# Moving modulation units, weight roundings and partial additions in a two-layer hybrid mixer block

## The chip, the cores and the metric

The kernel runs on one core of one Trainium2 chip. The metric is the device time of one execution in microseconds (us). A core has a matrix engine (PE, with its weight load PEld), a vector engine (DVE), a scalar engine (ACT), GpSimd (POOL) and a sync engine (SP) that here issues nearly all loads. Each engine executes its own instructions in order and waits at semaphores for the others.

## The reference, cut to what matters

Two layers run over 512 latent and 256 context tokens of width 1024. In each, a condition vector gives six modulation vectors by one large product; four mixers (differential attention DA, the gated recurrence HG, neighbourhood attention NA, windowed attention SW) take a quarter of the width each; their outputs go through `w_out`; a squared-ReLU MLP follows. All matrices are fp32.

```python
for layer in range(DEPTH):
    mod_l = adaln_params(c, w_mod[layer], b_mod[layer])      # silu(c) @ w_mod + b, split in 6
    p_l = split_cols(modulate(x, norm1_g[layer], mod_l[0], mod_l[1]) @ w_in[layer])
    ...                                                      # the same for the context
    a_l, a_c = diff_attention(...)                           # DA
    b_l, b_c = hgrn2_mixer(...)                              # HG, a scan over chunks of 64
    n_l, n_c = neighbourhood_attention(...)                  # NA
    w_l, w_c = window_gqa(...)                               # SW
    x = x + mod_l[2] * (jnp.concatenate([a_l, b_l, n_l, w_l], axis=-1) @ w_out[layer])
    x = x + mod_l[5] * squared_relu_mlp(modulate(x, norm2_g[layer], mod_l[3], mod_l[4]), ...)
```

Within HG a step of the scan needs, for 64 positions, scores with a decay `exp(cum[t] - cum[s])` inside each chunk, and the state product `k * exp(last - cum)` against the values:

```python
new_state = exp(last)[..., None] * state + einsum('bhsk,bhsv->bhkv', kc * exp(last[:, :, None] - cum), vc)
rel = where(lower, cum[:, :, :, None, :] - cum[:, :, None, :, :], -inf)
scores = einsum('bhtk,bhsk,bhtsk->bhts', qc, kc, exp(rel))
```

## The kernel before, in words

**Units.** Weights are handled in units of 256 output columns (1 MB, 0.75 MB for the units of `w_out` named `outA`). All units stand in one list. A unit is loaded by SP into one of two `raw` buffers, by turns, so the load of a unit is issued when the unit two places ahead in the list is done with its buffer: a modulation unit when its product has run, a split unit when its low part is made. A split unit (all but the modulations) is rounded by ACT (`whi`, L1410), its rest is made by POOL (`wlo`, L775, or by DVE), and PE multiplies three times. ACT takes up each rounding at a point of its own instruction order, in `after_unit`, and there waits until the load has landed: everything behind it on ACT waits too.

**Modulation units.** `("mod", l, j, i)` is column block i of modulation j of layer l. Its `row` is 16 small PE matmuls (L918), DVE copies the result to `mrow` (L1908), its `turn` is 4 tiny matmuls (L923) and one addition on DVE (L1912). They are filler work: `fill_plan` deals them, with the chunks of the next mixer's projections, into the slots of a mixer. PE runs a slot's work within one step of that mixer; DVE and ACT have their parts at fixed points of theirs.

**DA** has a step for each of 24 units of attention in layer 0 (16 in layer 1), and one slot for each, with one more at the end. On PE a step is the scores of the next unit (L1096), the transposes of this one (L1113), the slot, and every second step the product with the values (L1133). After the last step ACT squares the output (`DA_y`, L1632), PE averages it (L1161), and ACT, DVE and PE norm it. In ACT's order the last two roundings of units that the slots let through stand ahead of these squares.

**HG** runs over tiles of 128 positions, 6 in layer 0 and 4 in layer 1. A tile has 6 levels (distances 1, 2, 4, ... 32) and a diagonal. For a level PE makes differences of `cum` (L1206, L1207), four levels ahead of where it stands; ACT takes their exponentials (L1721, two levels at once); DVE multiplies them with q (`HGx_qd`, L2313) and POOL with k (`HGx_kd`, L762); PE makes the scores (L1246); DVE masks them into `HG_at` (L2324). The exponentials have two rooms, each of two levels. A slot follows on PE behind the differences of each level. The roundings of the first two units of `w_out`, `outA` 0 and 1, are let through by the last two modulation rows of the slots, and ACT takes a slot up behind the exponentials of level (slot + 4) or (slot + 3).

**Behind the levels** PE multiplies with `outA` in chunks (L888 to L890; 512 and 256 columns by turns in layer 0, 512 in layer 1) that alternate between two banks of PSUM; DVE adds a finished chunk to `xT` (`add`, L2464) and so frees its bank. At the same time DVE makes, for each head h, `kdiff(h)` (L2369) and, after ACT's exponential (L1742), `kscale(h)` (L2375). PE transposes the scaled keys (L1279) once all four heads are done.

## Time and profile before

| | us |
|---|---|
| median of 3 runs | 2327.4 |
| lowest and highest of them | 2324.64, 2330.38 |
| the profiled execution, device time | 2326.89 |
| its span in the trace | 2325.1 |
| PE busy | 2087.4 (90%) |
| DVE, ACT, POOL busy | 1017.4, 785.0, 688.7 |

The profiled execution lies 0.5 us below the median, and 1.8 us of it lie outside its span. A row of the timeline has the start of an instruction (or of a run of equal ones) in us from the span's start, its duration in us, engine, line, operation, output and inputs, the count, and in square brackets how long the engine sat idle before it and what it waited for.

### The profile page before, as it was taken

What the parts mean: (1) busy time and instruction counts of PE and PEld (TensorE: products, weight loads), DVE (VectorE), ACT (ScalarE), POOL (GpSimd) and SP (SyncE); (2) the same over time, 40 slices, a digit from 0 to 9 for tenths busy, and PEclk for the clock granted to TensorE, in tenths of its full rate; (3) what the DMA queues carried; (4) which work ended last, traced back from release to release, by engine and by line L of the source; (5) the groups of instructions that cost most, each with busy time, mean ns of one, the idle gap of its engine ahead of it and who ended that gap; (6) DMA issues with size and microseconds to landing.
All of it is one profiled execution on the core that took longest, in us unless ns stands there. A gap on an engine that the chain in (4) does not pass through costs nothing.

```text
span 2325.1 us, 32051 instructions
## 1 busy us (share of the span) xinstructions
PE 2087.4 (90%) x13292; PEld 1743.4 (75%) x13292; DVE 1017.4 (44%) x1791; ACT 785.0 (34%) x1283; POOL 688.7 (30%) x567
## 2 busy tenths in 40 slices
PE   5799898879878899999999988998978888999998
PEld 3678786757667788888888876777767767778787
DVE  2545547844665641222213353445846755121222
ACT  1533323423425531222213153223434355232231
POOL 0231211010760223223232222223013713444542
PEclk9899998979999999999999998998989979999999
DMA  8220000551311111211212123010351312322222
GB/s 282 50 70 20 31 25 21 180 145 46 109 59 40 55 55 55 73 55 60 68 55 73 55 44 75 19 37 19 107 129 52 119 37 64 100 91 91 91 91 73
DMA packets 178352, 169.72 MB, mean 73 GB/s; under 512 B 29392, under 2 KB 174752, under 8 KB 178080
## 3 DMA queue, kind: packets, MB, share of 16 engines
q1 hardware_dynamic: 175840, 161.12, 22.6%
q10 hardware_dynamic: 2368, 6.55, 0.9%
q8 instruction: 106, 1.74, 0.3%
q14 instruction: 38, 0.31, 0.0%
HBM read 159.79 MB, written 2.10 MB: 70 GB/s over the span
## 4 chain that ended last, share of the span: by engine, by line
PE 74%; DVE 10%; ACT 6%; issue 4%; DMA 3%; POOL 2%; SPq 2%; DVEq 0%; ACTq 0%; POOLq 0%
PE gp L864 52%; PE sp L1096 3%; POOL HGx_kd L762 2%; PE gp L1133 2%; PE tp L1113 1%; SPq L710 1%; DVE small L2165 1%; PE sp L1087 1%; PE gp L888 1%; PE sp L1246 1%; ACT nt L1444 1%; PE gp L918 1%; PE sp L937 1%; PE sp L997 1%; DMA raw<-in_w_mod 1%
## 5 line engine op out<-in xcount | busy, mean ns | idle before, releaser
L775 POOL TENSOR_TENSOR wlo<-raw,whi 128x512 fp32r<-128x512 f32 x386 | 511.4, 1356 | 1338.6 <-ACT whi L1410 1338.4
L864 PE MATMUL gp<-xhi,whi 128*128 128x512 f32 (+1 forms) x1424 | 521.8, 366 | 36.2 <-DVE xlo L1954 21.4
L864 PE MATMUL gp<-xhi,wlo 128*128 128x512 f32 (+1 forms) x1424 | 507.8, 357 | 0.0
L864 PE MATMUL gp<-xlo,whi 128*128 128x512 f32 (+1 forms) x1408 | 504.2, 358 | 0.0
L864 PEld LDWEIGHTS gp<-xhi,whi 128*128 128x128 f32 x1424 | 278.0, 195 | 84.1 <-issue 11.3
L1410 ACT ACTIVATE whi<-raw 128x2048 fp32r<-128x2048 f32 (+1 forms) x100 | 187.2, 1873 | 401.6 <-PE gp L864 356.4
L864 PEld LDWEIGHTS gp<-xhi,wlo 128*128 128x128 f32 x1424 | 277.1, 195 | 39.4
L864 PEld LDWEIGHTS gp<-xlo,whi 128*128 128x128 f32 x1408 | 274.4, 195 | 38.5 <-issue 2.0
L864 PE MATMUL gp<-hhi,whi 128*128 128x512 f32 (+1 forms) x768 | 276.8, 360 | 9.6 <-issue 5.0
L864 PE MATMUL gp<-hlo,whi 128*128 128x512 f32 (+1 forms) x768 | 275.2, 358 | 0.0
L864 PE MATMUL gp<-hhi,wlo 128*128 128x512 f32 (+1 forms) x768 | 274.8, 358 | 0.0
L2464 DVE SCALAR_TENSOR_TENSOR xT<-gp,mods,xT 128x512 f32<-128x512 f32 (+1 forms) x140 | 90.4, 654 | 374.7 <-PE gp L864 362.6
L2528 DVE TENSOR_TENSOR frel<-frel 128x512 f32<-128x512 f32 (+1 forms) x98 | 71.1, 726 | 244.4 <-ACT frel L1456 244.4
L864 PEld LDWEIGHTS gp<-hhi,whi 128*128 128x128 f32 x768 | 145.1, 189 | 37.0 <-DVE xT L2464 7.4
L864 PEld LDWEIGHTS gp<-hhi,wlo 128*128 128x128 f32 x768 | 145.2, 189 | 22.7
L864 PEld LDWEIGHTS gp<-hlo,whi 128*128 128x128 f32 x768 | 145.2, 189 | 22.2
L1456 ACT ACTIVATE frel<-gp 128x512 f32<-128x512 f32 (+1 forms) x98 | 50.5, 518 | 198.5 <-PE gp L864 198.5
L2165 DVE TENSOR_REDUCE small<-sp 128x1 f32<-128x768 f32 (+4 forms) x120 | 90.0, 792 | 42.4 <-PE sp L1096 42.4
L2530 DVE TENSOR_TENSOR hlo<-frel,hhi 128x512 fp32r<-128x512 f32 (+1 forms) x98 | 65.8, 671 | 60.7 <-ACT hhi L1873 60.7
L1246 PE MATMUL sp<-HGx_qd,HGx_kd 128*128 128x128 f32 x480 | 69.5, 290 | 19.1 <-DVE HG_at L2324 12.8
L1246 PEld LDWEIGHTS sp<-HGx_qd,HGx_kd 128*128 128x128 f32 x480 | 60.6, 198 | 29.5 <-issue 20.9
L1873 ACT ACTIVATE hhi<-frel 128x512 fp32r<-128x512 f32 (+1 forms) x98 | 54.3, 554 | 84.0 <-DVE frel L2528 84.0
(361 smaller groups left out, 3262.6 us busy)
## 6 DMA issues: line engine op xcount, KB each, us to landing
raw<-in_w_ff SPq DMA_DIRECT2D x64, 1024.0 KB, 5.3
raw<-in_w_mod SPq DMA_DIRECT2D x48, 1024.0 KB, 5.2
raw<-in_w_in SPq DMA_DIRECT2D x20, 1024.0 KB, 5.3
raw<-in_w_in SPq DMA_DIRECT2D x24, 256.0 KB, 4.8
bias<-e SPq DMA_DIRECT2D x96, 32.0 KB
raw<-in_w_out SPq DMA_DIRECT2D x12, 256.0 KB, 2.9
xin<-in_x ACTq DMA_DIRECT2D x1, 2048.0 KB, 9.9
raw<-in_w_out SPq DMA_DIRECT2D x16, 128.0 KB, 3.4
```

Source lines behind the costliest of these rows:

```text
L762: ins = nc.gpsimd.tensor_tensor(o, i0, dv[r, :, :, side, :], ALU.mult)
L775: nc.gpsimd.tensor_tensor(wlo[:, s % 2, ks, :], raw[:, index[splits[s]] % 2, ks, :], whi[:, s % 2, ks, :].bitcast(F32), ALU.subtract)\
L864: mm = pe.matmul(out, lhs, rhs, start=(i == 0 and j == 0), stop=(i == KT - 1 and j == 2))
L1096: mm = pe.matmul(region(m, n, j, o, o + w), ql if i == 2 else qh, kl if i == 1 else kh, start=(i == 0 and not added), stop=(i == 2))
L1246: mm = pe.matmul(sp_[:, idx % 2, P * h:P * h + P], kk, qq, start=True, stop=True)
L1410: nc.scalar.activation(whi[:, s % 2, 0:k_tiles(v), :], raw[:, index[v] % 2, 0:k_tiles(v), :], ACT.Copy)\
L1456: nc.scalar.activation(frel[:, e % 2, 0:b - a], bank(n)[:, 0:b - a], ACT.Relu).then_inc(bank_free[group_bank[n]], 1)
L1873: nc.scalar.activation(hhi[:, 2 * j + c[0], a:b], frel[:, e % 2, 0:b - a], ACT.Copy)\
L2165: V.tensor_reduce(small[:, c + j:c + j + 1], scored(m, n, j, w), AX.X, ALU.max, negate=True)\
L2464: ins = V.scalar_tensor_tensor(out=xT[:, k, a:b], in0=bank(n)[:, 0:b - a], scalar=mods[:, l, 8 * gate_chunk + k, MOD_COL[c[1]]:MOD_COL[c[1 ...
L2528: V.tensor_tensor(r, r, r, ALU.mult).then_inc(ls(l, "h_sq"), 1)
L2530: V.tensor_tensor(hlo[:, 2 * j + c[0], a:b], r, hhi[:, 2 * j + c[0], a:b].bitcast(F32), ALU.subtract)\
```

## The change

Three edits, no instruction added or taken away.

1. **The plan.** `counts` says how many modulation units each mixer's slots get. DA goes from 16 to 14 in layer 0 and from 9 to 7 in layer 1, HG from 8 to 10 and from 7 to 9.
2. **ACT's roundings in HG** follow their slot by 7 or 8 levels instead of 3 or 4, and what is left over is done at the end.
3. **DVE behind the levels** runs `add(0)` behind `kdiff(1)` instead of behind `kdiff(3)`, and, in layer 0, `add(1)` behind `kdiff(3)` instead of behind `kscale(3)`.

```diff
-    counts = {("NA", 0): 0, ("SW", 0): 0, ("DA", 0): 16, ("HG", 0): 8, ("NA", 1): 0, ("SW", 1): 0, ("DA", 1): 9, ("HG", 1): 7}
+    counts = {("NA", 0): 0, ("SW", 0): 0, ("DA", 0): 14, ("HG", 0): 10, ("NA", 1): 0, ("SW", 1): 0, ("DA", 1): 7, ("HG", 1): 9}
...
-                    if level >= 4:
-                        fill(ENDS["HG", l][level - 4])
-                        fill(ENDS["HG", l][level - 3])
+                    if level >= 8:
+                        fill(ENDS["HG", l][level - 8])
+                        fill(ENDS["HG", l][level - 7])
...
-                for slot in ENDS["HG", l][-5:]:
+                for slot in ENDS["HG", l][-9:]:
                     fill(slot)
...
                 kdiff(0)
                 kdiff(1)
+                add(0)
                 kscale(0)
                 kdiff(2)
                 kscale(1)
                 kdiff(3)
-                add(0)
+                if not last:
+                    add(1)
                 kscale(2)
                 kscale(3)
-                if not last:
-                    add(1)
```

What the plan gives, worked out from `fill_plan` (r is a row, t a turn, tok a chunk of 128 tokens of the projection HGi, which PE takes 24 matmuls for; a unit's turn stands in the slot behind its row, at its head):

| slots | before | after |
|---|---|---|
| DA 0, slots 21 to 24 | t r; t tok5; r; t r t | t r; t tok5 r; t r; t |
| DA 1, slots 13 to 16 | r; t tok5; r; t r t | the last eighth of tok4, r; t tok5 without its last eighth; that, r; t |
| HG 0, slots with rows | 0 3 6 10 13 16 20 23 | 0 2 5 8 10 13 16 18 21 24 |
| HG 1, slots with rows | 0 2 5 7 10 12 15 | 0 2 4 6 8 10 12 14 16 |

The units that follow DA's last two rows in the buffers are `HGf0` and `HGf1`, each loaded in four pieces of 64 columns. In layer 1 their loads are let go by the rows of slots 13 and 15, before by those of slots 15 and 16; in layer 0 by those of slots 22 and 23, before 23 and 24.

ACT in HG of layer 0, around levels 22 to 32. `whi` with 1536 columns is the rounding of `outA` 0 and then of `outA` 1, `mix<-tp` and `mix<-op` read the output of a finished tile out, `HG_tmp` and `HGx_exps` are the two rooms of the exponentials:

```order
 L1721 ACTIVATE HG_tmp<-sp,cf 128x2x2x128 x2
-L1410 ACTIVATE whi<-raw 128x1536
-L1721 ACTIVATE HGx_exps<-sp,cf 128x2x2x128 x2
-L1410 ACTIVATE whi<-raw 128x1536
+L1721 ACTIVATE HGx_exps<-sp,cf 128x2x2x128 x2
 L1712 ACTIVATE cum_hi<-sp 128x512
...
+L1410 ACTIVATE whi<-raw 128x1536
+L1721 ACTIVATE HGx_exps<-sp,cf 128x2x2x128 x2
+L1721 ACTIVATE HG_tmp<-sp,cf 128x2x2x128 x2
+L1410 ACTIVATE whi<-raw 128x1536
```

The first rounding moved from behind the exponentials of level 24 to behind those of 28, the second from 26 to 32. In layer 1 they go from 16 to 22, the last pair of levels, and from 18 to behind the last read-out.

ACT at the end of DA in layer 1; `whi` with 2048 columns is the rounding of `HGf0` and `HGf1`, `DA_pt` the copy of the last unit's transposes, `DA_y` the squares:

```order
 L1600 ACTIVATE DA_p,small<-sp,small 128x768 x2
-L1610 ACTIVATE DA_pt<-tp 128x384
-L1410 ACTIVATE whi<-raw 128x2048 x2
+L1410 ACTIVATE whi<-raw 128x2048
+L1610 ACTIVATE DA_pt<-tp 128x384
+L1410 ACTIVATE whi<-raw 128x2048
```

The rounding of `HGf0` moved ahead of the copy of the last transposes. In layer 0 ACT's order there is the same as before.

DVE behind the levels in layer 0; L2369 is `kdiff`, L2375 `kscale`, L2464 `add`:

```order
 L2369 TENSOR_TENSOR HG_tmp<-HG_cum,HG_ref 128x768 x2
+L2464 SCALAR_TENSOR_TENSOR xT<-gp,mods,xT 128x512
 L2375 TENSOR_TENSOR HG_k<-HG_k,HG_tmp 128x768
 L2369 TENSOR_TENSOR HG_tmp<-HG_cum,HG_ref 128x768
 L2375 TENSOR_TENSOR HG_k<-HG_k,HG_tmp 128x768
 L2369 TENSOR_TENSOR HG_tmp<-HG_cum,HG_ref 128x768
-L2464 SCALAR_TENSOR_TENSOR xT<-gp,mods,xT 128x512
+L2464 SCALAR_TENSOR_TENSOR xT<-gp,mods,xT 128x256
 L2375 TENSOR_TENSOR HG_k<-HG_k,HG_tmp 128x768 x2
-L2464 SCALAR_TENSOR_TENSOR xT<-gp,mods,xT 128x256
```

`add(0)` moved ahead by four instructions, `add(1)` by two.

## Rows read from the trace of the kernel before

**Rows 1.** The page, part 4: shares of the chain that ended last

```profile
PE 74%; DVE 10%; ACT 6%; issue 4%; DMA 3%; POOL 2%; SPq 2%; DVEq 0%; ACTq 0%; POOLq 0%
```

**Rows 2.** The timeline of PE, end of DA in layer 0

```profile
495.75 1.07 PE L918 MATMUL gp<-raw,silu_c 128*32 128x256 f32 x16
...
499.68 0.58 PE L923 MATMUL gp<-cf,mrow 128*128 128x2 f32 x4 [0.64 <-DVE mrow L1908]
511.22 5.25 PE L1161 MATMUL sp<-cf,DA_y 128*128 128x2 f32 x24 [10.97 <-ACT DA_y L1632]
```

**Rows 3.** The timeline of ACT, the same place

```profile
503.93 1.91 ACT L1410 ACTIVATE whi<-raw 128x2048 fp32r<-128x2048 f32 x1 [7.90 <-DMA raw<-in_w_in]
508.44 1.91 ACT L1410 ACTIVATE whi<-raw 128x2048 fp32r<-128x2048 f32 x1 [2.60 <-DMA raw<-in_w_in]
```

**Rows 4.** The timeline of SP (SPq), ends of DA in layers 0 and 1

```profile
496.88 14.36 SPq L721 DMA_DIRECT2D raw<-in_w_in  x9
...
1712.38 14.31 SPq L721 DMA_DIRECT2D raw<-in_w_in  x9
```

**Rows 5.** The timelines of PE and ACT, end of DA in layer 1

```profile
1701.37 1.07 PE L918 MATMUL gp<-raw,silu_c 128*32 128x256 f32 x16
...
1711.24 1.07 PE L918 MATMUL gp<-raw,silu_c 128*32 128x256 f32 x16
...
1719.37 1.91 ACT L1410 ACTIVATE whi<-raw 128x2048 fp32r<-128x2048 f32 x1 [7.86 <-DMA raw<-in_w_in]
...
1725.76 1.13 ACT L1632 ACTIVATE DA_y<-mix 128x512 f32<-128x512 f32 x2
```

**Rows 6.** The timeline of ACT, roundings among the levels, layers 0 and 1

```profile
652.74 1.48 ACT L1410 ACTIVATE whi<-raw 128x1536 fp32r<-128x1536 f32 x1 [2.89 <-DMA raw<-in_w_out]
...
661.73 1.48 ACT L1410 ACTIVATE whi<-raw 128x1536 fp32r<-128x1536 f32 x1 [6.35 <-DMA raw<-in_w_out]
...
1830.55 1.49 ACT L1410 ACTIVATE whi<-raw 128x1536 fp32r<-128x1536 f32 x1 [1.22 <-DMA raw<-in_w_out]
...
1837.02 1.48 ACT L1410 ACTIVATE whi<-raw 128x1536 fp32r<-128x1536 f32 x1 [3.31 <-DMA raw<-in_w_out]
```

**Rows 7.** The timeline of PE, what follows the second rounding, layers 0 and 1

```profile
665.20 2.05 PE L1246 MATMUL sp<-HGx_qd,HGx_kd 128*128 128x128 f32 x8 [5.90 <-DVE HG_at L2324]
...
1839.13 0.39 PE L1206 MATMUL sp<-dif,cum_hi 128*128 128x256 f32 x1 [1.17 <-ACT HG_tmp L1721]
```

**Rows 8.** The timeline of PE: first scores of tiles 0, 1, 3, 4, 5; layer 1: 0, 1

```profile
592.67 1.13 PE L1246 MATMUL sp<-HGx_qd,HGx_kd 128*128 128x128 f32 x8 [0.34 <-POOL HGx_kd L762]
...
606.92 1.06 PE L1246 MATMUL sp<-HGx_qd,HGx_kd 128*128 128x128 f32 x8
...
639.20 1.07 PE L1246 MATMUL sp<-HGx_qd,HGx_kd 128*128 128x128 f32 x8
...
657.77 1.06 PE L1246 MATMUL sp<-HGx_qd,HGx_kd 128*128 128x128 f32 x8
...
677.33 1.06 PE L1246 MATMUL sp<-HGx_qd,HGx_kd 128*128 128x128 f32 x8
...
1791.53 1.13 PE L1246 MATMUL sp<-HGx_qd,HGx_kd 128*128 128x128 f32 x8 [0.61 <-POOL HGx_kd L762]
...
1806.63 1.06 PE L1246 MATMUL sp<-HGx_qd,HGx_kd 128*128 128x128 f32 x8
```

**Rows 9.** The timelines of DVE and PE behind the levels, layer 0

```profile
696.70 0.96 DVE L2375 TENSOR_TENSOR HG_k<-HG_k,HG_tmp 128x768 f32<-128x768 f32 x1
...
700.43 0.75 DVE L2464 SCALAR_TENSOR_TENSOR xT<-gp,mods,xT 128x512 f32<-128x512 f32 x1
...
703.07 0.48 DVE L2464 SCALAR_TENSOR_TENSOR xT<-gp,mods,xT 128x256 f32<-128x256 f32 x1
...
701.23 0.80 PE L888 MATMUL gp<-mix_hi,whi 128*128 128x512 f32 x1 [4.91 <-DVE xT L2464]
...
707.33 0.60 PE L1279 MATMUL tp<-cf,HG_k 128*128 128x128 f32 x4
```

## The prediction, made before the changed kernel ran

> **What bounds the kernel now.** I read the chain that ended last first: 74% of it is PE and 10% DVE [rows 1]. So PE's own work decides nearly everywhere, and a change can pay in two ways: less PE work on the path, or fewer gaps on PE. Of the gaps I read the timelines of the three stretches that the diff touches, PE first and then the engine that it waited for.
>
> At the **end of DA** PE sits idle 10.97 us in layer 0 before the averages, waiting for ACT's squares [rows 2]. ACT had waited for two loads and rounded both units, and only then squares, from 508.44 + 1.91 = 510.3 [rows 3], though PE has no more attention to do from 500.3. The reader is to see a fixed sequence: row done (495.75 + 1.0), load issued at 496.88 [rows 4], landed at 503.93, which is 7.05 us after the issue, the next landed at 508.44, 4.51 later, its rounding 1.9, squares. In layer 1 it is the same: issue 1712.38, first landed 1719.37, squares 1725.76 [rows 4, 5]. **Among the levels** ACT waits for the loads of `outA` 0 and 1: 2.89 and 6.35 us in layer 0, 1.22 and 3.31 in layer 1 [rows 6]. The exponentials queued behind stop the levels, and after the second one PE has been idle 5.90 us and makes its 8 scores in 2.05 us instead of 1.06 [rows 7, 8]: they run at the clock's lower level, 1.2 GHz, after that idle time, the others at 2.4. **Behind the levels** in layer 0 PE waits 4.91 us for `add(0)`, which ends at 701.18, because its third chunk needs that bank [rows 9].
>
> **Part A, the end of DA in layer 0.** Removed are two units. A row takes 1.07 us and a turn 0.58 [rows 2], each with the end of its last matmul, which the next instruction overlaps; back to back I take 1.0 and 0.4, 2.8 for two units. Steps with a chunk in their slot are bound by PE, steps with a row alone partly by ACT and DVE, so not all of it counts: 2.8 less at most, some 2 at least. On the other side slot 22 now ends with a row, and DVE finishes the last unit's probabilities only after the chunk of that slot; this delays the last row, not the one before it. The load of `HGf0` goes out after the row of slot 22, which directly follows tok5; before, the last transposes stood between (0.3 us). So the issue comes 2.8 + 0.3 = 3.1 us earlier. The second load lands 4.5 us after the first wherever it is issued soon enough. Everything to the squares moves with it. **A = -3.0, between -2 and -4.** If the cover were gone (all of the removed work hidden anyway) it would be -0.3.
>
> **Part B, the end of DA in layer 1.** Here the load of `HGf0` is let go in slot 13, two steps earlier, and its rounding stands ahead of the last copy of ACT. What is left is the load of `HGf1`, let go by the row in slot 15. That row ended at 1711.24 + 1.0 = 1712.2 [rows 5]; with one unit fewer before it, of 1.4 us, and what remained idle in the steps without a chunk, it ends at about 1711.0. A load alone took 7.05 us from its issue (1719.37 less 1712.38 is 6.99 here), so it lands at 1711.1 + 7.0 = 1718.1, the rounding takes 1.9, the squares begin at 1720.0 instead of 1725.76. **B = -5.7.** If `HGf1` arrives at the 4.51 us that it took behind the first, it is -8.2; if nothing of the unit removed shows, -4.5. The wait that is added on ACT ahead of the last copy: the row of slot 13 ended at 1702.4 [rows 5], a unit less makes it 1701.0, the load lands at 1708.1, the rounding ends at 1710.0. The last transposes end about where the row behind them began, 1711.24 less 1.2; so the copy, and PE's last product, which stands behind the row, lose 0 to 0.5 us, and the squares, later than both, lose nothing.
>
> One rule of the Trainium skill speaks to the load. A load of 1 MB alone took 6.99 and 7.05 us, and one of two on the way 4.51 [rows 3 to 5]. The Trainium skill, page "DMA: Bandwidth & Descriptors", section "Measured (HBM→SBUF, 128 partitions, SWDGE, issued from GpSimd)" and the fit above it, gives about 2.0 us plus the bytes at 436 GB/s, an estimate of 4.4 us for this load; by it B would be some 2.6 us larger. The measured 7 us decide here.
>
> **Part C, the levels of layer 0.** Three terms. (1) Tile 0 gets one unit more, rows in slots 0, 2, 5 instead of 0, 3. Layer 1 has exactly these slots now: its tile 0 takes 1806.63 - 1791.53 = 15.10, layer 0's 606.92 - 592.67 = 14.25 [rows 8]. So +0.85, which is less than the unit's 1.4 on PE, since POOL and the rooms of the exponentials leave gaps. (2) Tile 3 has two units before and after but loses the wait for `outA` 0. Tiles 1 and 2, also with two, take (639.20 - 606.92) / 2 = 16.1, tile 3 took 657.77 - 639.20 = 18.6: -2.4. (3) Tile 4 took 677.33 - 657.77 = 19.6 with one turn; it gets one unit more and loses the wait for `outA` 1 with the slow clock behind it. I take 15.4, between tile 0 (14.25) and tiles 1 and 2 (16.1): -4.2. The moved roundings (1.48 each) stay on ACT behind levels 28 and 32; the loads are let go by slots 21 and 24. ACT runs four levels ahead of PE, so it reaches 28 when PE is at 24, three levels of 16.1 / 6 = 2.7 us behind slot 21: 8.1 us, which covers even the 7.0 of the loads in DA. For the second it is four levels. **C = 0.85 - 2.4 - 4.2 = -5.8, between -3 and -8.**
>
> **Part D, the levels of layer 1.** Tiles 1 and 2 get one unit more each, 2 x 0.85 = +1.7. ACT's waits of 1.22 + 3.31 = 4.5 us go; on PE only 1.17 shows [rows 7], where layer 0's 9.2 gave 5.90 and more. I take -2.0, between -1.2 and -4.1 (0.9 of the wait). The rounding of `outA` 1 falls behind the last read-out; POOL makes its rest some 4 us later, and PE needs it only in the third chunk, behind the keys: 0. **D = -0.3, between -3 and +2.5.**
>
> **Part E, behind the levels of layer 0.** `add(0)` would start at 696.70 and end at 697.45 instead of 701.18 [rows 9]. PE's third chunk starts there, 3.7 us earlier, after a gap of 1.2 us, so its 18 matmuls stay at the full clock; I put them at 4.2 us, against the 6.1 from 701.23 to 707.33, the first part of which ran at the lower one (0.80 for the first matmul), and the chunk ends at 701.7. What is late next is the fourth `kscale`: it ended with the start of `add(1)`, 703.07; `add(1)` ahead of it makes it 703.5. PE transposes the keys at 703.5 instead of 707.33. **E = -3.8, between -2.5 and -4.5.** In layer 1 PE's next work is the keys, whatever the order, and the sum of DVE's work ahead of them is the same: 0.
>
> **The sum.** -3.0 - 5.7 - 5.8 - 0.3 - 3.8 = -18.6 us. From the profiled execution's 2326.9 that is 2308.3; it lay 0.5 below the median, so I say **2308.8**. The ends of the parts would give 2301 and 2319.
>
> **The rivals.**
>
> *The lone load is fast.* If `HGf1` lands 4.5 us after its issue, B is -8.2 and the time 2306.3. For it: 4.51 between two landings; against: both lone ones took 7. Chance 0.12. It is also what the skill's page would say.
>
> *The levels charge each unit in full.* A unit in the levels holds DVE too, which waits for row and turn before the next product. If a unit costs 1.4 on PE and 1.1 of waiting on DVE, 2.5 instead of 0.85, four units cost 6.6 more: 2315.4. Against it stands the comparison of the two tiles 0. Chance 0.14.
>
> *DA was not bound by PE.* Then units taken out leave gaps, A is -0.3 and B -4.5: 2312.7. For it: the steps without a chunk have such gaps. Chance 0.12.
>
> *The change does not do what it says.* If the waits for the loads only hid other waits and `add(0)` came free no sooner, the levels would pay four units of 0.85, 3.4, and gain nothing, and E would be 0: 2326.9 - 8.7 + 3.4 + 0.5 = 2322.1. Chance 0.07. Against it: 5.90 us of PE's gap end on the chain through ACT's second rounding [rows 6, 7].
>
> *Slower: the loads cannot follow.* In layer 1 rows now stand in every second level. A load is issued when the row two ahead is done, so so it has four levels, 10.8 us. If loads took longer among each other, each of the 7 rows behind the second would wait for the rest: from 13.5 us a load the 7 waits of 2.7 use up the whole gain, and that is the point from which it decides; at 14.6 us it is 26.6 us and the kernel at 2335.4. Against: the slowest load in the rows took 7.05. Chance 0.02.
>
> **How the numbers follow.** Forecast 0.53, rivals 0.12, 0.14, 0.12, 0.07, 0.02. 0.3% (7 us) is about what a measurement of this kernel can tell from no change, so the bounds are 2320.4 and 2334.4. The first three rivals lie below 2320.4: faster 0.91; same 0.07 (the fourth); slower 0.02 (the last). The range that holds 8 in 10 reaches from the best ends of the parts to the worst: 2301 to 2318.
>
> **What would show it right or wrong.** PE's idle time before the averages of DA: about 11 us again in layer 0 at a start near 508, and 7 to 8 instead of 10 in layer 1. ACT's roundings among the levels without a wait for the load. Tile 0 of layer 0 at 15.1, tiles 3 and 4 near 16. PE's wait for `add(0)` about 1 us, a new one of some 1.8 us for `kscale`. Wrong would be: a wait for `in_w_mod` on PE in layer 1's levels, or the roundings still waiting, or tiles 1 and 2 of layer 1 over 17 us.

## The result, and the profile after

The changed kernel takes 2313.57 us (median of 5 runs, 2309.11 to 2316.44), the kernel before beside it 2328.87 us: 15.3 us less. The ratio of the two groups of runs, as the record computes it (near the ratio of the medians, not equal to it), is 0.9929, with a 95% interval of 0.9906 to 0.9952. Measured a second time beside other kernels it was 2310.60 against 2330.31, ratio 0.9918 (0.9904 to 0.9932). The prediction was 2308.8 with a range of 2301 to 2318, and "faster" with 0.91, by its own bound of 0.3%; both ratios lie beyond that bound.

The profiled execution took 2315.06 us, its span is 2313.2. The shares of the chain that ended last, to be read beside [rows 1]: PE up 2 points, issue, DMA and POOL down 1 each.

```profile
PE 76%; DVE 10%; ACT 6%; issue 3%; DMA 2%; SPq 2%; POOL 1%; DVEq 0%; ACTq 0%; POOLq 0%
```

The ends of DA in layers 0 and 1, PE and ACT together (start, duration, engine, line, what, and in brackets the idle time before it with its cause). They answer to [rows 2, 3, 5].

```profile
375.49 0.49 PE L1096 MATMUL sp<-DA_hi,DA_hi 32*128 32x512 f32 x2 [1.14 <-DVE small L2146]
...
496.16 1.07 PE L918 MATMUL gp<-raw,silu_c 128*32 128x256 f32 x16
498.14 0.30 PE L1113 MATMUL tp<-cf,DA_p 128*128 128x128 f32 x1 [0.91 <-DVE DA_p L2182]
...
505.30 1.91 ACT L1410 ACTIVATE whi<-raw 128x2048 fp32r<-128x2048 f32 x1 [6.54 <-DMA raw<-in_w_in]
509.12 1.91 ACT L1410 ACTIVATE whi<-raw 128x2048 fp32r<-128x2048 f32 x1 [1.91 <-DMA raw<-in_w_in]
511.91 5.26 PE L1161 MATMUL sp<-cf,DA_y 128*128 128x2 f32 x24 [10.64 <-ACT DA_y L1632]
...
1610.27 0.49 PE L1096 MATMUL sp<-DA_hi,DA_hi 32*128 32x512 f32 x2 [0.39 <-DVE small L2146]
...
1699.18 1.07 PE L918 MATMUL gp<-raw,silu_c 128*32 128x256 f32 x16
...
1707.35 1.91 ACT L1410 ACTIVATE whi<-raw 128x2048 fp32r<-128x2048 f32 x1 [8.12 <-DMA raw<-in_w_in]
1709.92 0.34 PE L1161 MATMUL sp<-cf,DA_y 128*128 128x2 f32 x1 [7.67 <-ACT DA_y L1632]
```

Read by the clock on the wall, layer 0's averages start at 511.91 where they started at 511.22 [rows 2], as if part A had given nothing. That reading is wrong. This execution came late to the stage: its DA began at 375.49, that of the kernel before (profiled again) at 372.90, and in code that the change doesn't touch. What must be compared is the length of a stage, from its first row to its last:

```profile
372.90 0.50 PE L1096 MATMUL sp<-DA_hi,DA_hi 32*128 32x512 f32 x2 [1.14 <-DVE small L2146]
...
512.86 5.25 PE L1161 MATMUL sp<-cf,DA_y 128*128 128x2 f32 x24 [11.03 <-ACT DA_y L1632]
...
1620.94 0.50 PE L1096 MATMUL sp<-DA_hi,DA_hi 32*128 32x512 f32 x2 [0.38 <-DVE small L2146]
...
1726.41 3.55 PE L1161 MATMUL sp<-cf,DA_y 128*128 128x2 f32 x16 [9.98 <-ACT DA_y L1632]
```

So DA of layer 0 is 136.4 us where it was 140.0, and of layer 1 99.7 where it was 105.5. Much of such a late start comes from the first 160 us: in 14 traces of this study, one to a kernel or two, the first scores of NA attention in layer 0 start anywhere from 150.2 to 157.1 us, and DA 219.4 to 223.1 us behind them. Other stretches that no edit touches move too: from layer 0's MLP to the start of DA in layer 1 it is 746.3 to 753.2 us, and the two traces of deal_more differ there by 2.7. The stages in the table below repeat within 1.6 us in the three kernels that were traced twice. Which of these stretches makes up the spread of runs without a trace (4 to 13 us for one kernel) is not shown.

The levels of the changed kernel, first scores of each tile, which answer to [rows 8], and ACT's roundings of `outA` in layer 0, which answer to [rows 6] and now wait for no load:

```profile
591.81 1.13 PE L1246 MATMUL sp<-HGx_qd,HGx_kd 128*128 128x128 f32 x8 [0.34 <-POOL HGx_kd L762]
606.90 1.06 PE L1246 MATMUL sp<-HGx_qd,HGx_kd 128*128 128x128 f32 x8
...
656.60 1.06 PE L1246 MATMUL sp<-HGx_qd,HGx_kd 128*128 128x128 f32 x8
663.45 1.49 ACT L1410 ACTIVATE whi<-raw 128x1536 fp32r<-128x1536 f32 x1
669.28 1.48 ACT L1410 ACTIVATE whi<-raw 128x1536 fp32r<-128x1536 f32 x1
669.39 0.83 PE L1246 MATMUL sp<-HGx_qd,HGx_kd 128*128 128x128 f32 x6
...
1775.71 2.05 PE L1246 MATMUL sp<-HGx_qd,HGx_kd 128*128 128x128 f32 x8 [0.50 <-POOL HGx_kd L762]
1792.96 1.07 PE L1246 MATMUL sp<-HGx_qd,HGx_kd 128*128 128x128 f32 x8
1810.82 1.07 PE L1246 MATMUL sp<-HGx_qd,HGx_kd 128*128 128x128 f32 x8
1827.84 1.06 PE L1246 MATMUL sp<-HGx_qd,HGx_kd 128*128 128x128 f32 x8
```

Layer 0: tile 0 took 606.90 - 591.81 = 15.1 us, tile 3 16.9 (it began at 639.67), tile 4 669.39 - 656.60 = 12.8, where it had been 19.6. Layer 1: tile 1 took 17.9 and tile 2 17.0 us, up from 15.7 and 14.6. Its tile 0 took 17.3 us at a mean granted clock of 0.88, and 15.7 us at 1.00 in after_again, the changed kernel's second trace: that is the whole difference between 69.8 and 68.2 in the table below.

Behind the levels of layer 0, which answers to [rows 9]:

```profile
688.69 0.75 DVE L2464 SCALAR_TENSOR_TENSOR xT<-gp,mods,xT 128x512 f32<-128x512 f32 x1
689.49 0.50 PE L888 MATMUL gp<-mix_hi,whi 128*128 128x512 f32 x1 [1.07 <-DVE xT L2464]
695.55 0.63 PE L1279 MATMUL tp<-cf,HG_k 128*128 128x128 f32 x4 [1.61 <-DVE HG_k L2375]
```

The wait for `add(0)` is 1.07 instead of 4.91 us, and the new wait for `kscale` is 1.61, both as forecast.

**Stages of every kernel**, in us, each from its own trace and between the same rows of PE. DA: first L1096 on `DA_hi` to first L1161 on `DA_y`. Levels: first L1206 to last L1228. To keys: from there to the first L1279. To norm: from there to the first L1161 on `HG_tmp`. To FF: from there to the first L864 on `hhi`, in layer 0 only. The last column is the ratio of the kernel's runs to those of the kernel before in the same comparison, with its 95% interval.

| kernel | DA 0 | levels 0 | to keys 0 | to norm 0 | to FF | DA 1 | levels 1 | to keys 1 | to norm 1 | ratio |
|---|---|---|---|---|---|---|---|---|---|---|
| before | 141.3 | 102.4 | 17.9 | 38.9 | 125.4 | 105.5 | 67.3 | 12.1 | 35.9 | 1 |
| before_again | 140.0 | 102.2 | 17.8 | 38.8 | 125.5 | 105.5 | 66.1 | 13.5 | 35.8 | |
| order_only | 140.2 | 102.1 | 14.0 | 41.9 | 125.5 | 103.8 | 67.0 | 13.4 | 35.9 | 0.9990 (0.9975 to 1.0004) |
| lag_only | 143.3 | 91.9 | 17.9 | 38.8 | 125.5 | 104.1 | 64.8 | 13.5 | 36.4 | 0.9962 (0.9950 to 0.9974) |
| counts_only | 138.0 | 101.2 | 18.4 | 38.9 | 125.4 | 99.8 | 68.7 | 13.5 | 36.0 | 0.9951 (0.9936 to 0.9966) |
| no_counts | 140.4 | 91.9 | 14.0 | 42.0 | 123.9 | 104.0 | 64.4 | 13.5 | 35.1 | 0.9932 (0.9910 to 0.9954) |
| changed | 136.4 | 95.3 | 14.0 | 44.6 | 123.9 | 99.7 | 69.8 | 12.9 | 36.5 | 0.9929 (0.9906 to 0.9952) |
| after_again | 136.8 | 95.3 | 14.0 | 44.6 | 123.9 | 99.9 | 68.2 | 12.9 | 36.5 | 0.9918 (0.9904 to 0.9932) |
| keep_busy | 137.9 | 95.4 | 13.9 | 41.6 | 123.9 | 100.1 | 68.2 | 12.8 | 36.1 | 0.9922 (0.9901 to 0.9944) |
| mixed | 141.2 | 91.9 | 14.0 | 41.9 | 123.9 | 99.0 | 68.4 | 13.5 | 36.3 | 0.9942 (0.9920 to 0.9965) |
| deal_more | 133.4 | 97.3 | 14.0 | 40.4 | 125.4 | 97.2 | 69.3 | 12.9 | 36.5 | 0.9905 (0.9888 to 0.9923) |
| deal_more_again | 133.4 | 97.3 | 14.0 | 40.4 | 125.4 | 97.2 | 69.3 | 12.9 | 36.6 | 0.9886 (0.9869 to 0.9903) |
| deal_most | 128.8 | 101.5 | 14.0 | 40.4 | 125.4 | 95.6 | 72.7 | 12.9 | 36.1 | 0.9906 (0.9890 to 0.9922) |
| deal_more_busy | 130.4 | 97.3 | 14.0 | 40.4 | 125.4 | 96.2 | 69.3 | 12.8 | 32.9 | 0.9878 (0.9862 to 0.9893) |

### The profile page after: what moved, and what is told of

Read it like the earlier page. It is cut to its first block, busy times and chain, and to the rows that moved or that the text cites. A ratio compares the mean times of both kernels' runs of the same rounds, so it can differ in the third digit from the quotient of the medians.

```text
span 2313.2 us, 32050 instructions
## 1 busy us (share of the span) xinstructions
PE 2095.0 (91%) x13292; PEld 1745.8 (75%) x13292; DVE 1017.7 (44%) x1791; ACT 785.3 (34%) x1283; POOL 685.1 (30%) x567
## 4 chain that ended last, share of the span: by engine, by line
PE 76%; DVE 10%; ACT 6%; issue 3%; DMA 2%; SPq 2%; POOL 1%; DVEq 0%; ACTq 0%; POOLq 0%
PE gp L864 53%; PE sp L1096 3%; PE sp L1246 2%; PE gp L1133 2%; PE tp L1113 1%; PE gp L918 1%; SPq L710 1%; PE sp L1087 1%; POOL HGx_kd L762 1%; DVE small L2165 1%; ACT nt L1444 1%; PE gp L888 1%; PE sp L937 1%; PE op L1113 1%; PE sp L997 1%
## 5 line engine op out<-in xcount | busy, mean ns | idle before, releaser
L864 PE MATMUL gp<-xhi,whi 128*128 128x512 f32 (+1 forms) x1424 | 520.9, 366 | 36.2 <-DVE xlo L1954 21.4
L864 PE MATMUL gp<-xhi,wlo 128*128 128x512 f32 (+1 forms) x1424 | 507.5, 356 | 0.0
L864 PE MATMUL gp<-xlo,whi 128*128 128x512 f32 (+1 forms) x1408 | 503.5, 358 | 0.0
L864 PEld LDWEIGHTS gp<-xhi,whi 128*128 128x128 f32 x1424 | 277.7, 195 | 83.7 <-issue 11.3
L864 PEld LDWEIGHTS gp<-xhi,wlo 128*128 128x128 f32 x1424 | 276.6, 194 | 39.4
L864 PEld LDWEIGHTS gp<-xlo,whi 128*128 128x128 f32 x1408 | 274.2, 195 | 39.0 <-issue 2.0
L864 PE MATMUL gp<-hhi,whi 128*128 128x512 f32 (+1 forms) x768 | 275.9, 359 | 9.6 <-issue 5.0
L864 PE MATMUL gp<-hlo,whi 128*128 128x512 f32 (+1 forms) x768 | 274.2, 357 | 0.0
L864 PE MATMUL gp<-hhi,wlo 128*128 128x512 f32 (+1 forms) x768 | 273.9, 357 | 0.0
L2464 DVE SCALAR_TENSOR_TENSOR xT<-gp,mods,xT 128x512 f32<-128x512 f32 (+1 forms) x140 | 90.3, 653 | 373.8 <-PE gp L864 361.1
L864 PEld LDWEIGHTS gp<-hhi,whi 128*128 128x128 f32 x768 | 144.6, 188 | 37.0 <-DVE xT L2464 7.4
L864 PEld LDWEIGHTS gp<-hhi,wlo 128*128 128x128 f32 x768 | 144.6, 188 | 22.7
L864 PEld LDWEIGHTS gp<-hlo,whi 128*128 128x128 f32 x768 | 144.6, 188 | 22.3
L1246 PE MATMUL sp<-HGx_qd,HGx_kd 128*128 128x128 f32 x480 | 68.4, 286 | 13.6 <-DVE HG_at L2324 10.1
```

What stands on the lines that cost most here:

```text
L864: mm = pe.matmul(out, lhs, rhs, start=(i == 0 and j == 0), stop=(i == KT - 1 and j == 2))
L1246: mm = pe.matmul(sp_[:, idx % 2, P * h:P * h + P], kk, qq, start=True, stop=True)
L2464: ins = V.scalar_tensor_tensor(out=xT[:, k, a:b], in0=bank(n)[:, 0:b - a], scalar=mods[:, l, 8 * gate_chunk + k, MOD_COL[c[1]]:MOD_COL[c[1 ...
```

## The experiments

**The kernel before, once more.** No edit.

> The kernel before, profiled once more, to see how far its stages move of themselves. If the stage times read from single traces can be trusted, every stage behind the first scores of NA attention (150.2 us in the first trace) lies within 1.5 us of the first trace's: 141.3 us for layer 0's DA attention, 102.4 for its levels, 17.9 to the keys, 38.9 from the keys to the norm; 105.5, 67.3, 12.1 and 35.9 in layer 1. The spread of the medians then sits ahead of 160 us. Rival: the stages the change touches spread by 3 us or more each, and single traces don't tell a term of 3 us.

Measured: layer 0's tail repeats to 0.1 us, DA of layer 1 to 0.1, the other touched stages to 1.2 to 1.4 us; none spreads by 3. A single trace tells a term of 2 us in these stages, which medians with a spread of 7 us do not. The one stage that had looked longer in the changed kernel, layer 1's keys (12.9 against 12.1), is 13.5 here: nothing is left to explain there. Still, 143.3 in lag_only and 130.4 beside 133.4 in deal_more_busy show that layer 0's DA sometimes moves by 3 us without an edit in it. Part of it is the clock: the mean granted clock over the stage is 0.89 in lag_only and 0.90 to 0.92 in the five other traces with this plan. DA of layer 1 moves as well: 105.5 twice here, but 103.8 to 104.1 in order_only, lag_only and no_counts, whose plan is the same.

**The additions alone.**

```diff
                 kdiff(1)
+                add(0)
                 kscale(0)
 ...
                 kdiff(3)
-                add(0)
+                if not last:
+                    add(1)
                 kscale(2)
                 kscale(3)
-                if not last:
-                    add(1)
```

> Only the first partial additions move between the key differences; plan and roundings are those of the kernel before. Theory (the prediction's term E): in layer 0 the time from the last weigh of the levels to the first transposition of the scaled keys falls from 18.2 us to about 14.4, nothing else moves, and the kernel is 3.8 us shorter. Rival (given back): the keys come earlier, but the stretch behind them runs at the lower level of TensorE's clock, as in the trace of the changed kernel (696.9 to 702.5 us), and the first pair of key steps takes about 7.0 us instead of 4.6; the kernel is 1.4 us shorter. In layer 1 both say no change (12.4 us from last weigh to keys), if it was POOL's roundings that stretched that stretch in the changed kernel; 13.2 us there if it is the moved addition itself.

Measured: 17.85 to 14.0 us ahead of the keys, which is the forecast -3.8 to the tenth, and 38.9 to 41.9 behind them. Three of the 3.8 us go back, as the rival said, and the ratio can't be told from 1. The granted clock shows where. The columns are: stretch, its length, busy us of PE, PEld, DVE, ACT and POOL, granted clock, share of the DMA engines, GB/s. First the kernel before (again), whose keys start at 707.35, then order_only, whose keys start at 706.09:

```profile
700.00:707.00 7.00, 5.68 (x17) 4.59 (x18) 4.66 (x7) 1.82 (x3) 0.00 (x0) 0.63 0.00 0
707.00:712.00 5.00, 4.75 (x46) 4.31 (x45) 0.10 (x1) 3.12 (x5) 0.00 (x0) 1.00 0.00 0
```

```profile
699.00:706.00 7.00, 4.45 (x18) 3.31 (x18) 6.84 (x9) 3.83 (x6) 0.00 (x0) 1.00 0.25 88
706.00:711.00 5.00, 4.66 (x32) 4.34 (x33) 1.08 (x2) 2.76 (x5) 0.00 (x0) 0.66 0.00 0
711.00:716.00 5.00, 5.00 (x35) 4.51 (x34) 1.62 (x2) 1.53 (x3) 0.00 (x0) 0.66 0.01 3
```

The stretch at the lower clock has moved from ahead of the keys, where it fell in part on PE's wait for `add(0)`, to behind them, where PE is busy almost all the time (4.66 and 5.00 of 5 us).

**The roundings alone.** `level >= 4`, `level - 4`, `level - 3`, `[-5:]` become 8, 8, 7, `[-9:]`.

> Only ACT's roundings of the output weights move eight levels behind their slot. Theory (term C and D without the units): ACT's 2.9 and 6.4 us waits for the load in layer 0 and its 1.2 and 3.3 us waits in layer 1 are gone; layer 0's tiles 3 and 4 go from 18.6 and 19.6 us to about 16 and 15, the levels of layer 0 are 6 to 8 us shorter and those of layer 1 about 2 us. The last rounding of layer 1 falls behind the last level, and the DVE steps there run beside POOL's; 0.7 us more from last weigh to keys. Sum about -8 us. Rival (the clock): tile 4's 19.6 us came from the lower clock at 657 to 677 us, not from the wait; then tile 3 gains 2 us, tile 4 stays within 1.5 us of 19.6, and the sum is about -3 us.

Measured: layer 0's levels -10.3 us, layer 1's -1.9; by the ratio the kernel is 8.9 us faster. The rival of the clock falls: tile 4 goes from 19.5 to 11.8 us, as long as tile 5 (12.1), which has no unit at all, and tile 3 from 18.5 to 15.9.

```profile
644.32 1.07 PE L1246 MATMUL sp<-HGx_qd,HGx_kd 128*128 128x128 f32 x8
660.23 1.06 PE L1246 MATMUL sp<-HGx_qd,HGx_kd 128*128 128x128 f32 x8
665.75 1.49 ACT L1410 ACTIVATE whi<-raw 128x1536 fp32r<-128x1536 f32 x1
668.27 1.50 ACT L1410 ACTIVATE whi<-raw 128x1536 fp32r<-128x1536 f32 x1
672.02 1.06 PE L1246 MATMUL sp<-HGx_qd,HGx_kd 128*128 128x128 f32 x8
684.10 0.39 PE L1228 MATMUL op<-HG_at,HG_v 128*64 128x128 f32 x4
```

The two roundings stand without a wait. ACT's waits were 2.89 + 6.35 = 9.2 us [rows 6], and the levels gave back 10.3: about all of the wait, and something on top. The slow clock behind the wait can account for it: over tile 4 the mean granted clock is 0.82 in the kernel before and 1.00 here. No run takes the two apart.

**The counts alone.** The dictionary of the plan: 14/10 and 7/9.

> Only the counts of the plan change (14/10 in layer 0, 7/9 in layer 1); roundings stay four levels behind, additions stay. Theory (terms A and B, with what the changed kernel's trace shows of the levels): DA attention with its closing loads is 3 to 5 us shorter in layer 0 and 5 to 8 us in layer 1; the two added units cost 0.9 to 2.5 us in all in layer 0's first tile and 4 to 5 us in layer 1's levels; the output weights are loaded later as well and their roundings wait 1 to 3 us more. Sum -4 to -7 us. Rival (every unit costs in the levels what it costs in the attention, 2.2 us each): four units cost 8.8 us there, and the sum is within 2 us of nothing.

Measured: -2.6 us in DA of layer 0 and -5.7 in layer 1 (against the mean of the two traces of before), -1.1 in layer 0's levels and +2.0 in layer 1's; -7.4 in all, and -11.4 by the ratio (-14.9 to -7.9). The trace is of the slowest of the six runs (2325.3 us against a median of 2317.8) and has 753.2 us in the untouched stretch ahead of DA in layer 1, 4 more than before; where the rest of the difference lies is open. The 7.4 us of the stages lie just above the 4 to 7 expected, although DA of layer 0 gave less than forecast, and the tiles of layer 0 show why its levels did not grow. Tiles 0, 1, 3 and 5 are longer by 0.9, 0.5, 1.8 and 1.0 us, but tile 4 falls from 19.5 to 14.4. The last row of the slots is now in slot 24, not 23, so by the counts alone ACT's second rounding moves from behind the exponentials of level 26 to behind those of 28, and it waits 0.78 us for its load instead of 6.4; the first rounding waits 5.46 instead of 2.8. PE's gap of 5.90 us [rows 7] is 0.33. So the counts take away part of the waits that the edit of the roundings takes away too, and this trace does not show that a unit is free where the levels wait.

**The change without the counts.** The two other edits on the plan of before.

> The additions and the roundings of the change on the plan of the kernel before (16/8 and 9/7). If the edits add up it is the sum of the two kernels above: about -11 us by the prediction's terms (-3.8 in layer 0's tail, -6 to -8 in layer 0's levels, -1 in layer 1's). By the theory that the dealt units gain, it is 4 to 7 us slower than the changed kernel (-15.3). By the rival that they bring nothing (their gain in the attention is paid back in the levels), it equals the changed kernel within 2 us; if it is faster, the dealing costs.

Measured: equal to the changed kernel by the ratio (0.9932 beside 0.9929 and 0.9918). The intervals reach 5 us to either side, but the traces agree: from the first scores of NA attention to the end it is 2159.7 us here, and 2159.0 and 2159.3 in the changed kernel. So the theory that the dealt units bring 4 to 7 us on top is not borne out. The changed kernel less this one, stage by stage: DA 0 -3.8, levels 0 +3.4, to norm 0 +2.6, DA 1 -4.2, levels 1 +4.6. With the waits gone, a unit costs 1.7 us in layer 0's levels and 2.3 in layer 1's, about what it saves in DA. The edits do not add up: alone, the counts bring 11.4 us and the two others 15.8, together 16.5 to 19. Tile 4 of layer 0 shows it: 19.5 us before, 14.4 with the counts, 11.8 with the roundings moved, 12.8 with both. The same wait can't be removed twice.

**Layer 0 without, layer 1 with the dealt units**, and layer 1's roundings back at four levels (`(8, 4)[l]` for 8).

> The changed kernel with layer 0's plan as before (16/8), layer 1's as changed (7/9), and layer 1's roundings back at four levels behind. Theory (where the levels have no slack, a unit costs there what it saves in the attention; where they still wait, it is free): layer 0's levels take 92 us (95.3 in the changed kernel) and its DA attention 141 (136.4); layer 1's DA attention 100 and its levels 68.7 instead of 69.8. Against the kernel before -15 to -16 us, as the changed kernel. Rival (units pay in layer 0): 4 us slower than the changed kernel, since layer 0's attention loses 4 to 5 us and the levels give back 1 us at most.

Measured: 2314.85 against 2328.74, ratio 0.9942, with the stages as the theory had them (91.9, 141.2, 99.0, 68.4), and 13.5 us below the kernel before by the ratio, a little less than the 15 to 16 expected. The ratio lies 0.0013 above the first one of the changed kernel, inside both intervals, and 0.0024 above the second, whose interval it misses; a kernel 3 to 6 us slower than the changed one isn't excluded by the ratios, only by the traces (2159.2 us from the first scores of NA attention to the end). It shows that layer 1's levels are as long with the roundings four levels behind as with eight once they hold 9 units.

**TensorE kept busy while it waits for the keys.**

```diff
+                spare = mix_high(MIX_ORDER[0])
+                for _ in range(20 if last else 6):
+                    pe.matmul(tp[:, 0:512], spare[:, 0:P], spare[:, 0:512], start=True, stop=True)
                 pe.wait_ge(*gupto("ke", 4))
                 keys(0)
```

> The changed kernel, and TensorE multiplies a settled operand into a bank that the key transpositions overwrite, 6 times in layer 0 and 20 times in layer 1, while it waits for the scaled keys; the rest is untouched. Theory (the clock takes back term E): the wait of 1.6 us ahead of the keys, with the 1.1 us before it, is what lowers the clock behind them; with the wait filled, the first key step takes about 4.6 us instead of 7.0, the stretch from keys to norm in layer 0 about 40 us instead of 44.6, and in layer 1 about 34.5 instead of 36.4 where the transpositions themselves now run at the lower level. Sum -4 to -6 us against the changed kernel. Rival: the clock falls for what TensorE did long before (or at a fixed time), the stretches stay at 44.6 and 36.4 within 1 us, and the kernel is as fast as the changed one or up to 2 us slower, if the added products run past the keys.

Measured: the clock behind layer 0's keys is 1.00, and the stretch to the norm 2.9 us shorter, yet longer than before's 38.8. The changed kernel first (keys at 695.55), keep_busy (keys at 693.19) second; the last row of each is the second stretch at the lower clock, some 20 us behind the keys:

```profile
688.00:695.00 7.00, 4.87 (x22) 3.53 (x20) 6.90 (x9) 4.01 (x6) 0.00 (x0) 1.00 0.31 99
695.00:700.00 5.00, 4.20 (x31) 3.88 (x32) 1.49 (x3) 2.71 (x6) 0.00 (x0) 0.72 0.00 0
700.00:705.00 5.00, 5.00 (x34) 4.60 (x34) 1.62 (x2) 1.40 (x3) 0.00 (x0) 0.60 0.01 3
...
715.50:725.50 10.00, 7.83 (x40) 6.05 (x39) 3.23 (x6) 4.83 (x10) 0.00 (x0) 0.61 0.34 107
```

```profile
686.00:693.00 7.00, 5.95 (x26) 4.43 (x24) 6.90 (x9) 4.00 (x6) 0.00 (x0) 1.00 0.26 97
693.00:698.00 5.00, 4.59 (x45) 4.26 (x45) 1.43 (x4) 3.14 (x6) 0.00 (x0) 1.00 0.00 0
698.00:703.00 5.00, 4.99 (x47) 4.07 (x47) 3.50 (x7) 2.48 (x5) 0.00 (x0) 1.00 0.01 3
...
713.20:723.20 10.00, 10.00 (x37) 7.74 (x38) 3.26 (x8) 4.51 (x10) 0.00 (x0) 0.53 0.14 42
```

The first stretch at the lower clock is gone. The second is not the first one come later: both kernels have it, and from 705.0 to 728.0 in the changed kernel and from 702.7 to 725.7 here the mean granted clock is 0.78 in either. The two layers gain 3.3 us in the trace, of the 4 to 6 expected; none of it can be told in the ratio.

**More units dealt.** `("DA", 0): 12, ("HG", 0): 12, ("DA", 1): 5, ("HG", 1): 11`.

> The changed kernel with two more units dealt from the attention to the levels in each layer (12/12 and 5/11). Theory (as above): layer 0's DA attention falls by another 3 to 4 us, layer 1's by 2 to 5 us; the levels grow by 3.4 us in layer 0 and by 5 us in layer 1; the sum is within 2 us of the changed kernel. By the prediction's terms (a unit costs 0.4 us in the levels and saves 1.5 to 2.8 us in the attention) it would be 7 us faster than the changed kernel. Rival: the loads can't follow in layer 1's levels, which then grow by 10 us or more.

Measured: ratio 0.9905. My theory of the break-even was wrong here. DA falls by another 3.2 and 2.6 us, and the levels grow by 2.0 in layer 0 and by 0.3 in layer 1 (by 1.1 against after_again, whose tile 0 ran at the full clock). What is behind layer 0's keys is 44.6 - 40.4 - 1.5 = 2.7 us shorter, with a mean granted clock of 0.96 to the norm instead of 0.81, though the code and the two waits ahead of the keys are those of the changed kernel. So only some 3 us of the gain are the units' own. The rival of the loads falls too: 11 units lengthen layer 1's levels by about 1 us, not by 10.

**The same beside the changed kernel, and further.** The second has 8/16 and 2/14, the third 12/12 and 5/11 with the 20 products of keep_busy in layer 1 alone.

> The changed kernel once more, beside the ones below. If the change is worth what the stage times of the traces say (6 to 7 us in layer 0's levels, 3 to 5 in each layer's DA attention, less 1 to 3 us in layer 1's levels, and layer 0's tail gaining 3.9 us ahead of the keys and losing 3 to 5.7 behind them), its median is 14 to 17 us below the kernel before. Rival: the first measurement was lucky or unlucky by its spread (7 us), and it is 12 or 19 us. In the trace, the clock behind layer 0's keys falls as in the first one (0.67 in the 5 us behind them) if the order of the additions sets it; it stays at 1.00 if it depends on more than this code.

> The kernel with two more units dealt in each layer (12/12, 5/11), again beside the changed kernel. Theory (the prediction's price holds: a unit saves 1.5 to 2 us in the attention and costs 1 us in the levels): 5 to 7 us faster than the changed kernel. Rival (pays what it saves): within 2 us of it, and the first measurement's 7 us were spread.

> 8/16 in layer 0 and 2/14 in layer 1. Theory (there is a point from which the levels take no more): the attention's savings end where it waits for its own chain of maxima, exponentials and turns rather than for units (133.4 us in layer 0 and 97.2 in layer 1 fall by 2 to 4 us at most), and 16 units over 27 slots and 14 over 18 slots lengthen the levels by 4 to 8 us in each layer; slower than 12/12 by 3 to 10 us. Rival (each unit still saves 0.7 us net): 4 to 5 us faster than 12/12. Second rival (the loads can't follow): 14 loads of 1 MB in layer 1's levels need more than the 69 us that these take, and they grow by over 10 us.

> 12/12 and 5/11, and TensorE multiplies a settled operand 20 times while it waits for layer 1's scaled keys (6 us), nothing in layer 0. Theory (the filled wait keeps the clock up over the keys): the granted clock in the 5 us behind layer 1's keys is 0.65 or more instead of 0.50, the stretch from keys to norm is 0.4 us shorter (36.1 against 36.5), and the kernel as a whole 0 to 1 us faster, which the medians can't tell. Rival (the fall comes later instead, as behind layer 0's keys with the wait filled): keys to norm is shorter, and a later stretch of the layer longer by the same.

Measured in one comparison: changed 2310.60, 12/12 2303.01, 8/16 2308.43, 12/12 with the products 2300.97 us. The changed kernel is 19.7 us below the kernel before, more than the 14 to 17 that I had expected from the stages. 12/12 is 7.6 us faster than the change, near what the prediction's price of a unit gives, but partly by luck: 2.7 us of it are the clock behind layer 0's keys, which that price does not have. Past it the levels pay: 8/16 and 2/14 save another 4.7 and 1.6 us in DA and cost 4.2 and 3.4 in the levels, 1.4 us lost of the 5.4 by which the medians differ (the intervals of the two ratios overlap), with no wait of the size of the second rival (14 units, 72.7 us; PE waits 1.4 us in all for loads of modulation weights there). The lowest median of the study is the last, 29.3 us below the kernel before and 9.6 below the changed one; the ratios do not tell it from 12/12 alone. There the clock stays up behind layer 1's keys; first deal_more_again, then deal_more_busy:

```profile
1847.00:1852.00 5.00, 5.00 (x28) 4.26 (x27) 0.52 (x1) 2.53 (x5) 0.00 (x0) 0.50 0.00 0
1852.00:1857.00 5.00, 5.00 (x29) 3.86 (x28) 1.44 (x2) 1.42 (x3) 0.00 (x0) 0.65 0.00 0
```

```profile
1842.00:1847.00 5.00, 4.46 (x35) 3.72 (x36) 1.38 (x4) 2.90 (x5) 0.00 (x0) 1.00 0.00 0
1847.00:1852.00 5.00, 5.00 (x50) 4.15 (x48) 2.72 (x6) 2.53 (x5) 0.00 (x0) 1.00 0.02 3
```

Keys to norm is 32.9 against 36.6 us, and what follows to the end is no longer for it (424.6 us, 424.0 and 425.2 in the two traces without the products), so the rival of a later fall is out. In keep_busy the same 20 products had left the clock at 0.65 and 0.67 in these two stretches, and won 0.4 us.

## Why the prediction was right

Against the mean of the two traces of before, with the mean of the two of the changed kernel, from the first scores of NA attention to the end (what lies ahead of them, which no edit touches, took 2.6 us more in the traces of the changed kernel):

| part | forecast | measured | |
|---|---|---|---|
| A, DA 0 | -3.0 (-2 to -4) | -4.0 | the row that lets the load of `HGf0` go starts 120.7 us into the stage, instead of 125.1 |
| B, DA 1 | -5.7 | -5.7 | the row of slot 15 starts 1.1 us earlier in the stage (forecast 1.2) |
| C, levels 0 | -5.8 (-3 to -8) | -6.9 | roundings -10.3, units +3.4 |
| D, levels 1 | -0.3 (-3 to +2.5) | +2.3 | roundings -2.1, units +4.4 |
| E, tail 0 | -3.8 | +0.3 | -3.8 ahead of the keys, +5.7 behind them, -1.6 to FF |
| rest of the kernel | 0 | -1.1 | -0.9 between DA and levels of layer 0, and spread |
| sum | -18.6 | -15.1 | |

The time fell into the range, but in part by luck: the terms D and E missed by 2.6 and 4.1 us, and larger gains in A, in C and in the rest of the kernel made up for 3.2 us of that. The ends of the parts, as stated, give 2299.7 and 2317.9 us and not the 2301 and 2319 of the prediction; the result lies inside either.

**A and B** held by their mechanism, less exactly than the table says. The six traces with 16 units in layer 0's DA have a mean of 141.1 us and the four with 14 units 137.3, so A is -3.8; the five with 9 units in layer 1's have 104.6 and the five with 7 have 99.7, so B is -4.9, and that -5.7 came out to the tenth is luck. In A the load goes out 4.4 us earlier and not 3.1, and the two loads together take 0.4 us longer. In B the chain is row, load, rounding, squares, and the load of `HGf1` alone took 1707.35 - 1700.2 = 7.1 us from the end of its row, so *the lone load is fast* is out. The fit in the Trainium skill, page "DMA: Bandwidth & Descriptors", section "Anatomy of one DMA — SWDGE (gpsimd) path", from which the estimate of 4.4 us was worked out, is not met here either; it is for transfers that GpSimd issues, and the same page's section "Measured (HBM→SBUF, 128 partitions, SWDGE, issued from GpSimd)" has 6.15 us for 1 MB. `HGf0` and `HGf1` are loaded in four pieces of 256 KB; loads of 1 MB in one piece land after a median of 5.1 to 5.3 us in the traces of before and after. *DA was not bound by PE* is out as well: DA 0 fell by 4.0 and by 3.2 more with the next two units.

**C and D** were near in their sum (-6.1 forecast, -4.6 measured) and wrong in two terms of opposite sign. The units were mis-sized: 0.85 us each came from the two tiles 0, where a third unit really costs 0.85 (14.24 to 15.1). In tiles 1 and 2 of layer 1 the third costs 2.2 us each (17.9 and 17.0 against the 15.7 and 14.8 of lag_only), near the 2.5 of *the levels charge each unit in full*. The sign I had named for it, tiles 1 and 2 over 17 us, is there. But that rival holds only in some tiles. In deal_more, against no_counts, a third unit costs 2.4 us in layer 0's tile 3 (18.4 against 15.9) but 1.0 in its tile 1 (17.6 against 16.6), and in layer 1 the fourth costs 0.3 us in tile 0 and 1.0 in tile 1, against after_again. Why the price differs by tile is not shown. The other term, the removed waits, was too small: I let tile 4 fall to 15.4 us, between tiles that hold units; it fell to 11.8, as long as tile 5. Where a wait goes, the tile to compare with is the one that has neither the wait nor the units.

**E** is the step that failed. All that it said of the keys came true (1.07 and 1.61 us of wait, 3.8 us earlier). What it left out is the clock behind the keys: it let the time at the lower clock ahead of them vanish and took the stretch behind them as unchanged. That stretch has the same 342 matmuls of PE in each kernel, and its length goes with its mean granted clock: 38.8 us at 1.00 (before), 40.4 at 0.96 (deal_more), 41.9 at 0.92 (order_only), 42.0 at 0.88 (no_counts), 44.6 at 0.81 (changed). order_only shows that the new order of the additions alone brings the first part of this, 3.0 us. The other 2.7 us come with a second stretch at the lower clock, some 20 us behind the keys, which order_only and lag_only do not have and no_counts, which joins their edits, has.

*The change does not do what it says* and *the loads cannot follow* are out by the rows of ACT and by 14 units in 72.7 us.

**What stays open** is what sets the place of the lower clock. The changed kernel, no_counts and deal_more run the same instructions with the same two waits ahead of layer 0's keys, 4.5 of 7 us busy, and had 0.67, 0.70 and 1.00 in the 5 us behind them, each within 0.02 of that in its repeat where there is one. The filled wait gave 1.00 in layer 0 in its one trace, and in layer 1 0.65 and 1.00. So the wait alone does not decide. What ran before it may, and no run here separates the two.

## What to carry to other kernels

Compare the lengths of stages, not the times at which they end: here one trace reached the changed code 5.6 us later than the other (375.5 against 369.9), which hid a gain of 4. Price a moved unit at the place where it lands, with the waits there as they will be after the other edits, and look for what moves with it: here the counts alone shifted a rounding by two levels, which took 5.6 us off one wait and put 2.6 on another. With the waits gone a unit cost 1.7 to 2.3 us, about what it had saved. And a gap of PE that closes ahead of the critical step isn't won before the clock behind that step has been read.

## What the runs showed of the hardware

**The place of the lower clock.** Shortening the wait for `add(0)` from 4.91 to about 1.1 us moved the stretch at the lower of the two levels (1.2 GHz; a granted clock of 0.63 over 7 us, then 0.66 over 10) from one side of layer 0's keys to the other, and 20 products that nobody reads, in a wait of 6 us, were worth 3.7 us in one kernel and 0.4 in another. What the lower clock costs shows in a stretch of 342 matmuls: 38.8 us at a mean granted clock of 1.00, 44.6 at 0.81.

**VectorE beside GpSimd.** Five copies of a few columns behind layer 1's levels take 0.16 to 0.22 us each where POOL is idle, as in the changed kernel, whose POOL starts at 1842.21. In the kernel before (profiled again), where POOL was 5.36 of 7 us busy from 1851.5, three of the five take 1.21 to 1.26 us and two 0.18 and 0.21:

```profile
1840.99 0.16 DVE L2359 COPY HG_ref<-HG_cum 64x16 f32<-64x16 f32 x1
...
1841.98 2.93 DVE L2369 TENSOR_TENSOR HG_tmp<-HG_cum,HG_ref 128x768 f32<-128x768 f32 x2
1842.21 5.79 POOL L775 TENSOR_TENSOR wlo<-raw,whi 128x512 fp32r<-128x512 f32 x3 [1.69 <-ACT whi L1410]
```

```profile
1853.08 1.26 DVE L2359 COPY HG_ref<-HG_cum 64x16 f32<-64x16 f32 x1
...
1857.17 1.83 DVE L2369 TENSOR_TENSOR HG_tmp<-HG_cum,HG_ref 128x768 f32<-128x768 f32 x2
```

In the changed kernel the pair of key differences takes 2.93 instead of 1.83 us beside POOL, so what is won at the copies is partly lost there: the stretch to the keys is 12.9 us, and 12.1 and 13.5 in the two traces of the kernel before, of which the first has only two slow copies (0.99 and 1.22 us).
